# RMS norms applied behind the products instead of in front of them, in a one-core decoder step

## What is computed

```python
# layer 0
h = rmsnorm(x, norm_mix[0]);  z = gelu(h @ a_w_in);  u, v = split(z)
v = layernorm(v, ln_g, ln_b)                       # over 1024 channels
x = x + (u * (W_s v + b_s)) @ a_w_out              # mixing inside 128-token chunks
h = rmsnorm(x, norm_ffn[0]);  x = x + (silu(h @ Wg) * (h @ Wu)) @ Wd     # 2816 wide
# layer 1
kv = rmsnorm(x, kv_norm) @ w_kv                    # 1536 columns
proj = rmsnorm(x, norm_mix[1]) @ b_w_in            # 1024 queries, 48 gates
x = x + sparse_attention(proj, kv, caches) @ b_w_out
x = x + moe(rmsnorm(x, norm_ffn[1]));  y = rmsnorm(x, norm_final)
# rmsnorm(x, g) = x * rsqrt(mean(x*x) + eps) * g, the mean over the 1024 channels
```

## Time and profile before

| | us |
|---|---|
| median of 3 runs | 1410.26 (1409.53 to 1412.23) |
| the profiled execution | 1410.61 |
| its span | 1409.0 |
| PE busy in it | 1314.0 (93%) |
| DVE busy | 1053.0 (75%) |
| ACT busy | 904.0 (64%) |

### The profile page before, as it was taken

How to read it: one execution, slowest core, us unless ns; L and a number is a source line. 1 busy time by engine, 2 the same in 40 slices (tenths; PEclk the granted TensorE clock), 3 DMA queues, 4 the chain that set the end, 5 groups by cost and what they waited for, 6 DMA issues and landing times.

```text
span 1409.0 us, 21410 instructions
## 1 busy us (share of the span) xinstructions
PE 1314.0 (93%) x7252; PEld 1103.1 (78%) x7252; DVE 1053.0 (75%) x1532; ACT 904.0 (64%) x1337; POOL 73.8 (5%) x75
## 2 busy tenths in 40 slices
PE   5998999988998999839999999999999999999896
PEld 4988999988936677628888888888888788888684
DVE  5776555557413387549989899899898998998796
ACT  5545444444312287438888798788887987887683
POOL 0010000003200000020000000000000000001600
PEclk9999999998998899969999999999999999999999
DMA  8399544454663001649989899899899998998950
GB/s 323 140 385 408 187 180 180 178 196 165 203 203 120 1 1 40 290 160 416 384 334 418 345 378 413 322 416 394 334 415 362 364 415 324 409 396 323 377 195 31
DMA packets 59423, 392.02 MB, mean 278 GB/s; under 512 B 6654, under 2 KB 12930, under 8 KB 20770
## 3 DMA queue, kind: packets, MB, share of 16 engines
q1 hardware_dynamic: 50578, 354.29, 64.2%
q0 software_dynamic: 8784, 36.92, 7.1%
HBM read 367.93 MB, written 27.45 MB: 281 GB/s over the span
## 4 chain that ended last, share of the span: by engine, by line
PE 84%; DVE 7%; issue 3%; ACT 2%; POOL 2%; DMA 2%; POOLq 1%; ACTq 0%; DVEq 0%
PE bank L1669 15%; PE bank L1671 15%; PE bank L1670 15%; PE bank L1346 8%; PE bank L1347 8%; PE bank L1348 8%; PE bank L1455 2%; PE bank L1654 1%; DVE w_lo L1230 1%; PE bank L1474 1%; PE bank L1559 1%; PE bank L1532 1%; DVE rstd L830 1%; ACT w_hi L730 1%; PE bank L1520 1%
## 5 line engine op out<-in xcount | busy, mean ns | idle before, releaser
L1230 DVE TENSOR_TENSOR w_lo<-raw,w_hi 128x1024 fp32r<-128x1024 f32 x528 | 623.4, 1218 | 32.5 <-ACT w_hi L730 14.6
L730 ACT CAST w_hi<-raw 128x1024 fp32r<-128x1024 f32 x528 | 542.7, 1055 | 88.5 <-PE bank L1671 87.4
L1669 PE MATMUL bank<-w_hi,xg_hi 128*128 128x512 f32 x704 | 275.8, 392 | 0.6 <-DVE xg_lo L1236 0.6
L1671 PE MATMUL bank<-w_hi,xg_lo 128*128 128x512 f32 x704 | 275.0, 391 | 0.0
L1670 PE MATMUL bank<-w_lo,xg_hi 128*128 128x512 f32 x704 | 274.7, 390 | 0.0
L871 DVE TENSOR_TENSOR d_lo<-ring,d_hi 128x1024 fp32r<-128x1024 f32 x120 | 146.6, 1223 | 102.6 <-ACT d_hi L572 102.3
L1346 PE MATMUL bank<-hA_hi,d_hi 128*128 128x264 f32 x640 | 188.0, 294 | 20.2 <-DVE hA_lo L861 15.2
L1347 PE MATMUL bank<-hA_lo,d_hi 128*128 128x264 f32 x640 | 185.2, 289 | 0.0
L1348 PE MATMUL bank<-hA_hi,d_lo 128*128 128x264 f32 x640 | 184.9, 289 | 0.0
L572 ACT CAST d_hi<-ring 128x1024 fp32r<-128x1024 f32 x120 | 125.4, 1046 | 59.0 <-PE bank L1348 51.7
L1669 PEld LDWEIGHTS bank<-w_hi,xg_hi 128*128 128x128 f32 x704 | 132.7, 188 | 28.4 <-issue 1.0
(11 more groups left out here) (314 smaller groups left out, 1593.3 us busy)
## 6 DMA issues: line engine op xcount, KB each, us to landing
raw<-in_moe SPq DMA_DIRECT2D x264, 1024.0 KB, 6.6
ring<-in_wd SPq DMA_DIRECT2D x30, 2048.0 KB, 8.4
out_rows<-zeros POOLq DMA_DIRECT2D x1, 6656.0 KB, 62.6
slot_rows<-zeros POOLq DMA_DIRECT2D x1, 6144.0 KB, 44.9
xs<-slot_rows POOLq DMA_DIRECT2D x8, 512.0 KB, 3.6
out_rows<-yrow POOLq DMA_DIRECT2D x8, 512.0 KB, 7.8
arena<-in_cmp_pages POOLq DMA_DIRECT2D x16, 128.0 KB, 2.4
X2v<-in_cmp_pages POOLq DMA_DIRECT2D x16, 128.0 KB, 2.5
```

Of the source, the lines that this page charges most:

```text
L730: nc.scalar.copy(w_hi[:, i % NSPLIT, :], raw[:, u % NRAW, ITEM * (i % 2):ITEM * (i % 2) + ITEM])\
L1230: V.tensor_tensor(w_lo[:, i % NSPLIT, :], raw[:, (i // 2) % NRAW, ITEM * (i % 2):ITEM * (i % 2) + ITEM], w_hi[:, i % NSPLIT, :].bitcast(F3 ...
L1669: T.matmul(out, lhs_hi, hi, start=first, stop=False)
L1671: return T.matmul(out, lhs_lo, hi, start=False, stop=last)
```

## The change

1. The split activation of the norms before vu, gu, kv and q is now that of x times the norm's weight, without the root. ACT writes the rounded high part straight from x (`round_weighted`), DVE the low part in one operation (`rest_weighted`). In ao and dn both are done chunk by chunk as x grows, in `add_chunk`.
2. The reciprocal root multiplies results as they leave PSUM, on DVE: `scaled` for v, u and kv; gate and up each in gu; both halves of q; the gates. ACT's gelu, silu and sigmoid then read SBUF in place; ACT's copies of kv and of q's odd halves are gone.
3. The mean of the squares is taken by PE after the first or second product of the next stage, and two more weight items are cast and split before root and reciprocal. Squares go to a buffer of their own (`sqr`), LayerNorm's root to `ln_rstd`.
4. The first loads: vectors, weight item 0 alone (0.5 MB), x in two halves, then the rest of the first tile.
5. POOL's fills of zeros move behind the gate rows' DMA, in the attention. The masking of `w_s` moves into the v products, the first key copies behind kv's fifth scaling.

```diff
+        sqr = arena[:, 17700:17700 + KC * NT].rearrange("p (k t) -> p k t", t=NT)
...
+        ln_rstd = carve(NT)
...
-            sp.dma_start(x[:], xT).then_inc(x_in, 16)
             sp.dma_start(VE[:], vectors).then_inc(setup_in, 16)
+            sp.dma_start(ring[:, 0, 0:DITEM], wd[0][:, 0:DITEM]).then_inc(item_in, 16)
+            for half in range(2):
+                sp.dma_start(x[:, 4 * half:4 * half + 4, :], xT[:, 4 * half:4 * half + 4, :]).then_inc(x_in[half], 16)
...
+                    first = DITEM if n == 0 else 0
+                    sp.dma_start(ring[:, n % NSLOT, first:], wd[wn][:, first:]).then_inc(done, 16)
...
             pool.dma_start(past_out, state_win).then_inc(past_stored, 16)
-            pool.wait_ge(zeros_ready, 1)
-            for rows in (slot_rows.rearrange("b p n -> (b p n)"), out_rows[0:NO_ROW, :].rearrange("r n -> (r n)")):
-                rows = rows.rearrange("(p q n) -> p q n", p=P, n=256)
-                pool.dma_start(rows, zeros[:].unsqueeze(1).to_broadcast(list(rows.shape))).then_inc(rows_zeroed, 16)
...
             pool.wait_ge(gtok_ready, 2)
             pool.dma_start(grow[:], gsam[0:NS, :]).then_inc(grow_in, 16)
+            pool.wait_ge(zeros_ready, 1)
+            for rows in (slot_rows.rearrange("b p n -> (b p n)"), out_rows[0:NO_ROW, :].rearrange("r n -> (r n)")):
...
+                    if n == 0:
+                        act.wait_ge(item_in, 16)
+                    if n == 1 or n % 4 == 0 and n:
...
-            def round_normed(norm, dst):
-                for k in range(KC):
-                    act.wait_ge(norm_ready, 8 * norm + k + 1)
-                    nc.scalar.copy(dst[:, k, :], hB[:, k, :]).then_inc(h_hi_ready, 1)
-
-
-            act.wait_ge(x_in, 16)
+            def round_weighted(weight, k, dst, ready):
+
+                nc.scalar.activation(dst[:, k, :], x[:, k, :], ACT.Copy, scale=weight[:, k:k + 1]).then_inc(ready, 1)
+
+
+            act.wait_ge(setup_in, 16)
+            round_to("vu", -2)
             for k in range(KC):
-                nc.scalar.activation(hB[:, k, :], x[:, k, :], ACT.Square).then_inc(sq_ready, 1)
-            act.wait_ge(setup_in, 16)
+                if k % 4 == 0:
+                    act.wait_ge(x_in[k // 4], 16)
+                round_weighted(vector("mix0"), k, hA_hi, h_hi_ready)
+            round_to("vu", -1)
+            for k in range(KC):
+                nc.scalar.activation(sqr[:, k, :], x[:, k, :], ACT.Square).then_inc(sq_ready, 1)
+            round_to("vu", 1)
             std(1, 0)
-            round_to("vu", -1)
-            round_normed(0, hA_hi)
 
             for c in range(KC):
                 round_to("vu", c)
-                projected(act, "vu", c)
-                nc.scalar.activation(vT[:, c, :], B[c % 4][:, 0:NT], ACT.Gelu_apprx_tanh).then_inc(v_ready, 1)
+                act.wait_ge(v_scaled, c + 1)
+                nc.scalar.activation(vT[:, c, :], vT[:, c, :], ACT.Gelu_apprx_tanh).then_inc(v_ready, 1)
...
+                round_weighted(vector("ffn0"), c, hA_hi, h_hi_ready)
                 squares(1, c)
+            round_to("gu", 1)
             std(4, 0)
-            round_normed(1, hA_hi)
...
-                projected(act, "gu", 2 * f)
-                if f >= 2:
-                    act.wait_ge(hF_ready, f - 1)
-                nc.scalar.activation(sil[:, f % 2, :], B[2 * (f % 2)][:, 0:NT], ACT.Silu).then_inc(sil_ready, 1)
+                act.wait_ge(gate_scaled, f + 1)
+                nc.scalar.activation(sil[:, f % 2, :], sil[:, f % 2, :], ACT.Silu).then_inc(sil_ready, 1)
...
+                act.wait_ge(x_ready, KC + c + 1)
+                round_weighted(vector("kvn"), c, hA_hi, h_hi_ready)
                 squares(2, c)
+                round_weighted(vector("mix1"), c, hC_hi, q_hi_ready)
+            for c in range(KC):
+                round_weighted(vector("mix1"), c, hB, gate_in)
+            round_to("kv", 1)
             std(5, 0)
-            round_normed(2, hA_hi)
-            round_normed(3, hC_hi)
             for c in range(12):
                 round_to("kv", c)
-                projected(act, "kv", c)
-                nc.scalar.copy(kvT[:, c, :], B[c % 4][:, 0:NT]).then_inc(kv_ready, 1)
-
-            act.wait_ge(q_zero, 1)
             for c in range(KC):
-                half = 64 * ((c // 2) % 2)
                 round_to("q", c)
-                projected(act, "q", c)
-                nc.scalar.mul(Q[half:half + 64, 2 * c + 1, :], B[c % 4][64:128, 0:NT], HD ** -0.5).then_inc(q_odd, 1)
-            act.wait_ge(gp_done, 1)
-            nc.scalar.activation(gT[0:48, :], MISC[0:48, 0:NT], ACT.Sigmoid, bias=par("bgate")[0:48, :]).then_inc(sig_ready, 1)
+            act.wait_ge(gp_scaled, 1)
+            nc.scalar.activation(gT[0:48, :], gT[0:48, :], ACT.Sigmoid, bias=par("bgate")[0:48, :]).then_inc(sig_ready, 1)
...
+            nrest = [0, 0]
+
+            def rest_weighted(weight, k, hi, lo, which):
+
+                nrest[which] += 1
+                hi_done, lo_done = ((h_hi_ready, h_ready), (q_hi_ready, q_lo_ready))[which]
+                dve.wait_ge(hi_done, nrest[which])
+                V.scalar_tensor_tensor(lo[:, k, :], x[:, k, :], weight[:, k:k + 1], hi[:, k, :].bitcast(F32), ALU.mult, ALU.subtract)\
+                    .then_inc(lo_done, 1)
...
+            dve.wait_ge(setup_in, 16)
+            rest_to("vu", -2)
             for k in range(KC):
-                add_up(hB, k, sq_ready, k + 1)
-            dve.wait_ge(setup_in, 16)
+                rest_weighted(vector("mix0"), k, hA_hi, hA_lo, 0)
+            rest_to("vu", -1)
+            for k in range(KC):
+                add_up(sqr, k, sq_ready, k + 1)
+            rest_to("vu", 1)
             inv_std()
-            rest_to("vu", -2)
-            split_normed(0, vector("mix0"), hA_hi, hA_lo)
-            rest_to("vu", -1)
-
-            dve.wait_ge(spatial_in, 48)
-            upto = const("upto").unsqueeze(1).to_broadcast([P, 8, P])
-            V.tensor_tensor(wsT[:], w_s, upto, ALU.mult).then_inc(ws_ready, 1)
-            V.tensor_tensor(dg[0:NS], ident[0:NS, 0:NS].unsqueeze(1).to_broadcast([NS, 8, NS]),
-                            vector("w00")[0:NS, :].unsqueeze(2).to_broadcast([NS, 8, NS]), ALU.mult).then_inc(ws_ready, 1)
+
+            def scaled(to, stage, c, ready):
+                projected(dve, stage, c)
+                V.tensor_tensor(to, B[c % 4][:, 0:NT], rstd[:, :], ALU.mult).then_inc(ready, 1)
+
+            def u_scale(c):
+                scaled(uT[:, c, :], "vu", KC + c, u_scaled)
 
             for k in range(KC):
                 rest_to("vu", k)
-                add_up(vT, k, v_ready, k + 1)
+                scaled(vT[:, k, :], "vu", k, v_scaled)
+                if k:
+                    add_up(vT, k - 1, v_ready, k)
+                if k == 4:
...
                 V.tensor_tensor(vT[:, k, :], vT[:, k, :], mu[:, :], ALU.subtract).then_inc(ctr_ready, 1)
+            u_scale(0)
+            u_scale(1)
             for k in range(KC):
+                if k == 4:
+                    u_scale(2)
                 rest_to("vu", 9 + k // 4)
                 add_up(hB, k, csq_ready, k + 1)
+            u_scale(3)
             rest_to("vu", 12)
-            inv_std()
+            u_scale(4)
+            inv_std(ln_rstd)
             for k in range(KC):
                 if k == 5:
                     rest_to("vu", 13)
-                V.scalar_tensor_tensor(vT[:, k, :], vT[:, k, :], vector("lng")[:, k:k + 1], rstd[:, :], ALU.mult, ALU.mult)\
+                    u_scale(5)
...
+            u_scale(6)
+            u_scale(7)
...
+            def add_chunk(c, norm, stage, item, squared=sqr, rests=()):
 
                 rest_to(stage, item - 1)
                 projected(dve, stage, item)
                 V.tensor_tensor(x[:, c, :], x[:, c, :], B[c % 4][:, 0:NT], ALU.add).then_inc(x_ready, 1)
                 if c < KC - 1:
                     rest_to(stage, item)
+                for r in rests:
+                    rest_weighted(vector(r[0]), c, *r[1:])
                 add_up(squared, c, sq_ready, 8 * norm + c + 1)
                 rest_to(stage, item)
 
             for c in range(KC):
-                add_chunk(c, 1, "ao", c)
+                add_chunk(c, 1, "ao", c, rests=[("ffn0", hA_hi, hA_lo, 0)])
+            rest_to("gu", 1)
             inv_std()
-            split_normed(1, vector("ffn0"), hA_hi, hA_lo)
...
+                rest_to("gu", 2 * f)
+                projected(dve, "gu", 2 * f)
+                if f >= 2:
+                    dve.wait_ge(hF_ready, f - 1)
+                V.tensor_tensor(sil[:, f % 2, :], B[2 * (f % 2)][:, 0:NT], rstd[:, :], ALU.mult).then_inc(gate_scaled, 1)
                 rest_to("gu", 2 * f + 1)
-                projected(dve, "gu", 2 * f + 1)
-                dve.wait_ge(sil_ready, f + 1)
                 if f >= 2:
                     rest_hidden_row(f - 2)
+                projected(dve, "gu", 2 * f + 1)
                 if f >= 4:
```

(34 more changed lines are left out.)

70 lines of the change are left out of this document (31 added, 39 removed).

## The result

The changed kernel takes 1398.53 us (median of 8 runs, 1395.95 to 1405.8), the kernel before 1410.66 beside it (8 runs, 1409.09 to 1412.23): 0.9918 of its time, 95% interval 0.9901 to 0.9935. It is faster, by 12.1 us, half of the forecast 25, and above the range of 1379 to 1395. The profiled execution took 1399.27, with a span of 1397.7 against 1409.0.

What follows compares the result with a forecast made beforehand. PE was taken to bound the kernel, so only its waits and slow stretches pay. Terms 8.0-4.2+8.3-0.9-0.4+13.6+0.6=25.0, from a profiled 1410.6 (0.4 over the median of 1410.26), gave 1385.5 us; range 1379 to 1395.

Steps and rivals of the forecast that it cites:

- three signs of being wrong: The prediction is wrong if gu's pairs are longer, PE starts after 10, or key copies show 3 us each again.
- What bounds the kernel: TensorE (PE), 84% of the chain; a change pays only where PE stands or runs slowly.
- (c): Rival in gu: PE no longer the bound, loop 6.6 us, 17.5 us over 22 pairs, time 1403; chance 0.05.
- (d): Rival in gu: half clock, pairs 10.6 us, not 5.8; change loses from 5.3 pairs (25.0/4.8); half of them 1438; chance 0.03.
- the loss of 0.9 forecast: Inside gu: after the last pair a longer path sets dn's start, a loss of 0.9 us.
- Start: First loads to the end of product 7: PE starts at 7.9, gain 8.0 us, bounds 6 and 9.
- LayerNorm: LayerNorm stage in vu: sum complete at 48.3, transposes after the biases at 74.8, loss 4.2 us, bounds 2 and 6.
- Rival (b): At LayerNorm: PE stands 3.4 us before product 15 and the clock falls; 2 us, time 1387.5; chance 0.2.
- dn: Chunk-by-chunk work on x in dn: chunks 0 to 3 cost PE 0.4 us.
- kv: From dn to kv: kv 0 starts at 310.1 and kv 4 ends at 326.3; gain 13.6 us, bounds 11 and 15.
- rival (a): In kv: if kv is 0.8 late, key copies meet GpSimd's memset again; price 5 us, time 1390.5; chance 0.22.
- End of q and zeros: Product behind q comes 0.6 us earlier; moving the zeros gains nothing.

Runs made afterwards that it cites:

- e7: The changed kernel with ScalarE's wait for the vectors moved behind the cast of item 0: 1400.54 us.
- e12: Kernel with four edits (later memsets, scale before remainder, dn's waits by bank, last vu product's remainder moved forward), plus item 1 on its own transfer: 1394.14 us.
- e3: The changed kernel with VectorE's scale of each v chunk put ahead of the next item's remainder: 1396.39 us.
- e8: The changed kernel with the fills of zeros back in their old place on GpSimd's queue, in stage ao: 1402.28 us.
- the three edits: On the changed kernel: memsets behind kv product 6, v scales ahead of remainders, dn's first products waiting for their own bank's row; together 1386.62 us.
- e10: The changed kernel with the remainder for vu's last product moved ahead of LayerNorm's eight weightings: 1406.01 us.
- e1: The changed kernel with GpSimd's three memsets waiting for product 6 of stage kv: 1392.66 us.

## Why the prediction was wrong, step by step

Two of its three signs of being wrong are there: PE started after 10 (at 10.35), and a key copy was slow again, one of 6.01 us. Three steps failed, in LayerNorm, in kv and at the start, and a fourth, in dn, in some executions.

- **What bounds the kernel**: right. Two waits for a normed x and their cold stretches are gone. gu's first product ran behind ao's last without a wait, with its mean at 112.18, and gu's pairs take the 5.8 us forecast, so rivals (c) and (d) are out. The wait ahead of dn grew from 0.91 to 1.86, the loss of 0.9 forecast; with the table's 7.45 that makes 8.4 from ao to gu, for 8.3.
- **Start**, 6.0 for 8.0, on the edge of its bounds. The first product came at 10.35, not 7.9. Three terms were mis-sized: item 0 landed at 6.1 instead of 5.1; the table load of 1.28, which in the kernel before ran at 0.97, stood behind the wait for item 0; the rest of the tile landed at 12.95 instead of 11.3. By e7 the table load hardly counts. By e12 the third counts in part: with item 1 cast 0.8 earlier, the first mean came 0.5 and LayerNorm's sum 0.6 earlier. No run moves item 0's landing alone.
- **LayerNorm**, -7.3 for -4.2 (bounds -2 and -6). The step that failed is "the sum is complete at 48.3", 0.6 behind the end of product 8; it was 3.1 behind (41.71 to 44.80). The forecast took the scale of chunk 7 to come as soon as product 7 was there. The loop that it had itself worked out (2.96 for one product) puts a remainder ahead of each scale, so this one came at 41.33, behind the remainder of item 9 and 2.6 us behind its product, and the gelu, the remainder of item 10 and the last add followed. e3 shows it: with the order reversed the stand goes and the clock stays full behind it, for 3 us. Rival (b) had the clock fall at the other stand, ahead of the last product; it fell at both places in some executions and most expensively behind the second. The working also left out the last two u-scales and gelus, which stand ahead of the copies out of T0 and T1 (0.7 of the 7.3: transposes at 71.37 for 70.72, ao at 84.93 for 83.58).
- **dn**, -2.1 for -0.4. "Chunks 0 to 3 cost PE 0.4" is not what failed. The term of 0.9 ahead of it made PE's wait 1.86 instead of 0.91, and half clock followed in this execution, 1.5 us of loss (197.46 against 195.95), a price that the forecast gave only to waits of 3.4 and more. In executions in which the clock held (eight of the ten profiled ones with this wait), dn's term is 1.5 better: about -0.6.
- **kv**, +7.1 for +13.6. This is rival (a), word for word: "if kv is 0.8 late". ACT's multiply by a weight column took 0.42, not the 0.32 of the square, so the eight gate inputs lasted 3.35 instead of 2.5 (from 308.59 to 311.94). The split of kv 2 stood behind them, and the timeline of PE has a wait of 0.51 for the split of kv 1 and of 0.25 for that of kv 2. From the start of kv 1 to that of kv 2 it took 3.41 instead of 2.9. Product kv 4, whose scaling the copies follow, ended 17.4 behind dn's end for 16.5, and the copies came 0.9 late with it. They began 1.8 ahead of the memset, and need 2.1. That the gate inputs are the larger part of this is read from the timeline; no run has them shorter. Price forecast 5, measured 5.6. The forecast gave 0.22 to an event that the margin missed by 0.3 us, less than an error of 0.1 us in one unit price brings over eight operations, while its own bounds for that price (0.3 to 0.5) held the error: its chance should have been near a half, and the "upper end later by 1" should have had the 5 us behind it.
- **End of q and zeros**: right, 0.4 for 0.6, and nothing (e8).

With the memset moved, kv's term is 12.7 against 13.6; the milestones of the three edits give 5.6, 3.4 and 3.7, and the kernel with all three is 12.6 earlier behind q (367.67 against 380.30). So nearly all of the forecast 25 us can be had: 12 of them were taken back in three places by the order of work on an engine's queue or by a wait for more than is needed, and one or two lines put each right. The direction and the chance of faster were right. The range was too narrow because it took the misses of the terms as independent: the late start, the late sum and the late gate inputs all pushed one way, and one of them tripped a rival. Its own bounds for start, LayerNorm and kv add up to 1381 to 1392, not 1380 to 1391, and with the 1 for ACT's price and the 5 of rival (a) they reach 1398, above its upper end of 1395. (In rival (d), 25.0/4.8 is 5.2 pairs, not 5.3.)

## What to carry to other kernels

When a wait is taken out, list what next falls together in time on other engines, and see how far the margin (here 0.6 us) is from the error of the smallest unit price beneath it. In a loop whose engine is full, the order within one turn decides when its last result appears, though not its period. A stand that can't be avoided had better lie ahead of dense matmuls than right ahead of sparse ones: here 13 of 47 runs were high against 13 of 16, the 16 all on one chip.

## What the runs showed of the hardware

- The clock fell behind shorter stands than I had expected, and not in each execution. Behind the wait of 1.86 us at the start of dn it was half for 3.5 us in two profiled kernels and full in eight; behind the wait of 3.1 for LayerNorm's sum it was half in nine of ten; behind the wait of 2.7 in e10 it was half for over 20 us in the profiled run, and the times of five runs of six are of that size. The Trainium skill, page "TensorE: Matmul & The Clock Gate", section "Why this matters for your kernels", advises against idle gaps over about 3 us between bursts. The traces here differ: the clock fell behind a wait of 1.86 us in two of ten.
- Once half, the clock stayed so through all of a sparse stretch: in e10 from 73.0 to 96.8 us, past ao's first dense product at 92.44, though PE's waits in it were 1.4 us and less and the last ones came before 80.
- Eight copies of 64x128 beside a memset took 7.78 us instead of 2.08, while remainders of 128x1024, two inputs and 1.23 us, ran beside a memset of the same size (e1) at their usual time. The Trainium skill, page "SBUF — State Buffer", section "SBUF: two separate sides", has the copies in a two-port mode shut out by a GpSimd operation for its whole length; this trace agrees: the copy that took 6.01 us ended at 331.12, the last memset at 331.03.
- ACT's copy with a scale from a column takes 0.42 us at 128x264 in a row (3.35 for eight), its square 0.33 (2.62 for eight), on the same tile. The first ACT table load ran at 0.97 us in the two kernels with one wait in front of the first activation (the kernel before and e7) and at 6.13, behind both, in the changed kernel with two.
